# The adaLN modulation moved from VectorE to TensorE in a two-layer hybrid decoder trunk

## The reference

```
c_act = jax.nn.silu(c)
for l in range(DEPTH):                                    # DEPTH = 2
    mod = c_act @ ada_w[l] + ada_b[l]                     # (1024) @ (1024 x 6144)
    sh_m, sc_m, g_m, sh_f, sc_f, g_f = jnp.split(mod, 6, axis=-1)
    h = _rmsnorm(x, norm_mix_g[l]) * (1.0 + sc_m) + sh_m
    cols = h @ w_in[l]                                    # three groups of heads
    ...
    mix = jnp.concatenate([y_a, y_b, y_c], axis=-1) @ w_out[l]
    x = x + g_m * mix
    h = _rmsnorm(x, norm_ffn_g[l]) * (1.0 + sc_f) + sh_f
    x = x + g_f * peer_ffn(h, peer_wq[l], peer_subkeys[l], peer_u[l], peer_v[l])
return _rmsnorm(x, final_norm_g)
```

## Time and profile before

| | |
|---|---|
| median of 3 runs | 1839.49 us (1839.48 to 1844.95) |
| profiled execution | 1839.77 us, its span 1837.9 us |
| TensorE clock, mean of what was granted | 0.851 of full speed |
| PE busy | 1314.2 us (72%) |
| DVE busy | 1398.9 us (76%) |
| ACT busy | 663.5 us (36%) |
| DMA | 706.42 MB, mean 384 GB/s |

### The profile page before, as it was taken

The page is one execution under the profiler, slowest core; times in us unless marked ns, Lnnn a source line. Parts: engine busy times, 40 slices in busy tenths (PEclk is TensorE's granted clock), DMA queues, the critical chain, the costliest instruction groups (busy, mean ns, idle before and its releaser), DMA issues.

```text
span 1837.9 us, 26377 instructions
## 1 busy us (share of the span) xinstructions
PE 1314.2 (72%) x9588; PEld 769.6 (42%) x9588; DVE 1398.9 (76%) x3327; ACT 663.5 (36%) x1634; POOL 517.6 (28%) x564
## 2 busy tenths in 40 slices
PE   2768787787877866787877867787877865555554
PEld 2657675453544534453444534443544531111111
DVE  5878588999974747999965748999965769985554
ACT  2313114444832233445732135336732233231112
POOL 2110012232332222232323232232422233343331
PEclk9875688897998987898988978898988977777777
DMA  9993669998999998999999999998999999999996
GB/s 393 421 396 139 229 240 403 401 415 352 361 420 421 421 420 355 383 414 367 400 421 421 420 420 372 393 422 339 378 421 421 421 421 420 404 405 421 421 421 261
DMA packets 97010, 706.42 MB, mean 384 GB/s; under 512 B 10992, under 2 KB 11504, under 8 KB 13296
## 3 DMA queue, kind: packets, MB, share of 16 engines
q0 software_dynamic: 80640, 587.24, 78.6%
q1 hardware_dynamic: 16240, 117.50, 15.7%
HBM read 703.64 MB, written 1.05 MB: 383 GB/s over the span
## 4 chain that ended last, share of the span: by engine, by line
DVE 43%; DMA 28%; PE 18%; issue 6%; ACT 4%; POOL 0%; DVEq 0%; ACTq 0%; POOLq 0%
DMA ringmem<-in_peer_uv_dram,eidx 23%; DVE ringmem L1451 15%; PE psum L785 5%; DMA W<-in_w_groups_dram 3%; PE psum L661 3%; PE psum L420 2%; DMA ringmem<-in_ada_pairs_dram 2%; DVE coef L1464 2%; DVE ringmem L1095 1%; PE psum L648 1%; DVE cand L1166 1%; DVE cand L1168 1%; DVE eid L1169 1%; DVE attn L1237 1%; DVE ast L1238 1%
## 5 line engine op out<-in xcount | busy, mean ns | idle before, releaser
L785 PE MATMUL psum<-ringmem,diag 64*64 64x512 f32 x4096 | 612.6, 724 | 280.8 <-ACT diag L1066 280.5
L387 POOL DMA_INDIRECT ringmem<-in_peer_uv_dram,eidx x512 | 492.0, 961 | 1082.3 <-PE psum L785 967.6
L1451 DVE SCALAR_TENSOR_TENSOR ringmem<-ringmem,psum 128x1024 f32<-128x1024 f32 x512 | 613.1, 1219 | 240.7 <-DMA ringmem<-in_peer_uv_dram,eidx 227.4
L785 PEld LDWEIGHTS psum<-ringmem,diag 64*64 64x64 f32 x4096 | 151.8, 154 | 605.8 <-ACT diag L1066 399.9
L1066 ACT ACTIVATE diag<-K,coef 128x128 f32<-128x128 f32 x512 | 176.5, 393 | 259.3 <-DVE coef L1464 258.9
L1058 ACT ACTIVATE coef<-dots 128x2 f32<-128x2 f32 x256 | 52.0, 203 | 509.9 <-DVE ringmem L1451 509.2
L420 PE MATMUL psum<-hT,W 128*128 128x128 f32 x1344 | 183.8, 298 | 40.4 <-DMA W<-in_w_groups_dram 22.1
L420 PEld LDWEIGHTS psum<-hT,W 128*128 128x128 f32 x1344 | 172.8, 210 | 83.5 <-issue 39.3
L1095 DVE SCALAR_TENSOR_TENSOR ringmem<-ringmem,diag 128x1024 f32<-128x1024 f32 x96 | 115.5, 1223 | 23.6 <-DMA ringmem<-in_ada_pairs_dram 21.4
L661 PE MATMUL psum<-hT,W 128*128 128x128 f32 x1024 | 126.1, 280 | 7.1 <-ACT hT L835 7.1
L661 PEld LDWEIGHTS psum<-hT,W 128*128 128x128 f32 x1024 | 120.1, 195 | 22.3 <-issue 12.2
(11 more groups left out here) (243 smaller groups left out, 1599.9 us busy)
## 6 DMA issues: line engine op xcount, KB each, us to landing
ringmem<-in_ada_pairs_dram POOLq DMA_DIRECT2D x48, 1024.0 KB, 18.4
W<-in_w_pieces_dram SPq DMA_DIRECT2D x48, 1024.0 KB, 9.4
W<-in_w_groups_dram SPq DMA_DIRECT2D x24, 1536.0 KB, 11.6
W<-in_w_groups_dram SPq DMA_DIRECT2D x12, 1024.0 KB, 9.7
ringmem<-in_peer_uv_dram,eidx POOLq DMA_INDIRECT x512, 14.9
W<-in_w_groups_dram SPq DMA_DIRECT2D x4, 1040.0 KB, 9.2
attn<-in_subkeys_t_dram SPq DMA_DIRECT2D x4, 1024.0 KB, 9.4
K<-in_consts_dram SPq DMA_DIRECT2D x1, 1546.0 KB, 18.3
```

What stands on the lines that cost most here:

```text
L387: nc.gpsimd.indirect_dma_start(slot(k), None, rows, bass.IndirectOffsetOnAxis(ap=eidx[:, ph % 2, m:m + 1], axis=0)).then_inc(row_landed[q ...
L785: mm = nc.tensor.matmul(acc_part(r, half), diag[d, k % DIAGS, d], slot(k)[d, D + half * 512:D + (half + 1) * 512], start=(k % SEL == 0), s ...
L1451: ins = v.scalar_tensor_tensor(out=u, in0=u, scalar=1.0, in1=hrep, op0=ALU.mult, op1=ALU.mult, accum_out=dots[:, j:j + 1])
```

## The change

The modulation is computed on PE instead of DVE. The columns of silu(c), now 128 x 8 numbers (`ccol`), stand in the array: for each of the 8 blocks of 128 inputs, one column of c is repeated over 32 columns of the array. A 1 MB slot now holds 128 inputs (partitions) by 2048 outputs; it passes as four matmuls of 512 columns, each in its own group of 32 columns of the array and so on its own 32 partitions of one PSUM bank. Eight slots make a group (`ADA_GROUPS` = 6): 2048 outputs, that is two sections of the modulation. After a group ACT copies the bank to SBUF (`ada_copy`), PE turns it with four 128 x 128 transposes (`ada_turn`), and DVE reads the sums as columns out of PSUM, adds the bias and folds in the gain (`modulation(g)`). The sections now come in the order in which they stand in `ada_w`.

The pace changes with it: 8 slots before segment 2 as before, then 0.5 slot per segment up to 28 (before: 0.65) and 0.9 after (before: 0.5 up to 56, then 0.75). All three engines follow this table in the lead. SP waits for the seventh slot instead of the sixth. c is loaded as 4 KB instead of 512 KB.

```diff
 def lead_pace():
-    due, out = 2.0 * KD, [1] * (2 * KD - 1) + [2]
+    due, out = 1.0 * KD, [0] * 3 + [1] * (KD - 3)
     for seg in range(2, SEGMENTS):
-        due += 1.3 if seg <= 28 else 1.0 if seg <= 56 else 1.5
-        out += [seg] * (int(min(due, ADA_CHUNKS)) - len(out))
-    return out + [SEGMENTS] * (ADA_CHUNKS - len(out))
+        due += 0.5 if seg <= 28 else 0.9
+        out += [seg] * (int(min(due, ADA_SLOTS)) - len(out))
+    return out
...
-        crow = diag[:].rearrange("p a c -> p (a c)")
+        ccol = diag[:, 0, 0:KD]
+        ada_row = diag[:, 1:5, :]
...
-                sp.dma_start(crow, c.broadcast_to([P, D])).then_inc(s["c_in"], 16)
+                sp.dma_start(ccol, c).then_inc(s["c_in"], 16)
...
-                sp.wait_ge(row_landed[5], 16)
+                sp.wait_ge(row_landed[6], 16)
...
-                Pace(mixing(0)).upto(END - 1)
+                def ada(q):
+                    g, k = divmod(q, KD)
+                    if k == 0 and g >= 2:
+                        pe.wait_ge(s["ada_copied"], g - 1)
+                    if q == 0:
+                        pe.wait_ge(s["c_ready"], 1)
+                    pe.wait_ge(row_landed[q % RING], 16 * (q // RING + 1))
+                    for b in range(4):
+                        mm = nc.tensor.matmul(bank[g % 2][32 * b:32 * b + 32, :], ccol[:, k:k + 1].broadcast_to([P, 32]),
+                                              ringmem[:, q % RING, b * 512:(b + 1) * 512],
+                                              start=(k == 0), stop=(k == KD - 1), skip_group_check=True)
+                    mm.then_inc(slot_free[q % RING], 1)
+                def ada_turn(g):
+                    pe.wait_ge(s["ada_copied"], g + 1)
+                    ...
+                    for j in range(4):
+                        tr = nc.tensor.transpose(bank[2 + g % 2][:, j * P:(j + 1) * P], ada_row[:, j, :], ident)
+                    tr.then_inc(s["ada_turned"], 1)
+                lead = Pace(mixing(0))
+                for q in range(ADA_SLOTS):
+                    lead.upto(LEAD[q])
+                    ada(q)
+                    if q == KD - 1:
+                        ada_turn(0)
+                    elif q % KD == 0 and q > KD:
+                        ada_turn(q // KD - 1)
+                lead.upto(LEAD[-1] + 1)
+                ada_turn(ADA_GROUPS - 1)
+                lead.upto(END - 1)
+                pe.wait_ge(s["mod_ready"], ADA_GROUPS)
                 place_h(0)
...
+                def ada_copy(g):
+                    act.wait_ge(slot_free[(KD * g + KD - 1) % RING], (KD * g + KD - 1) // RING + 1)
+                    if g:
+                        act.wait_ge(s["ada_turned"], g)
+                    nc.scalar.activation(ada_row.rearrange("p a c -> p (a c)"), bank[g % 2][:, :], ACT.Copy
+                                         ).then_inc(s["ada_copied"], 1)
...
-                def ada(j):
-                    q, a = divmod(j, 2)
-                    l, r = divmod(j, 6 * KD)
-                    dve.wait_ge(row_landed[q % RING], 16 * (q // RING + 1))
-                    u = ringmem[:, q % RING, a * D:(a + 1) * D]
-                    ins = v.scalar_tensor_tensor(out=u, in0=u, scalar=1.0, in1=crow, op0=ALU.mult, op1=ALU.mult,
-                                                 accum_out=MC[:, l, SECTIONS[r // KD], r % KD:r % KD + 1])
+                def modulation(g):
+                    l, a = g // 3, 2 * (g % 3)
+                    dve.wait_ge(s["ada_turned"], g + 1)
+                    ...
+                    sums = bank[2 + g % 2].rearrange("p (j b c) -> p b j c", j=4, b=4)[:, :, :, 0]
+                    step(v.tensor_tensor(part.rearrange("p (b j) -> p b j", b=4), sums,
+                                         b.rearrange("p (b j) -> p b j", b=4), ALU.add), *told)
+                    if scale:
+                        m = MC[:, l, scale, :]
+                        step(v.scalar_tensor_tensor(out=m, in0=m, scalar=1.0, in1=pcols[:, l, gain:gain + KD],
+                                                    op0=ALU.add, op1=ALU.mult), "mod_ready")
```

82 lines of the change are left out of this document (37 added, 45 removed).

## The result

The changed kernel takes 1851.65 us (median of 5 runs, 1850.61 to 1855.50) against 1840.29 for the kernel before (5 runs, 1839.48 to 1844.95): a ratio of 1.0061, with a 95% interval from 1.0045 to 1.0078. It is slower, by 11 us. The forecast was 1822 us, 17 us faster. Run once more on another chip, beside 27 runs of the kernel before (median 1841.30), the same kernel took 1847.22 us (10 runs, 1840.67 to 1852.64): ratio 1.0035, interval 1.0018 to 1.0052. So both times slower, by 6 to 11 us, and with a scatter of 12 us that the experiments explain only in part.

A forecast was written before the change was run, and what follows sets the result against it. The experts' rows bound the phases, so the lead's gain arrives one for one. Terms -0.5, -6, -12, -2.5, +1.5, +2.5 sum to -17.0 us: 1822 us, range 1806 to 1860 (the forecast's own 1806 to 1834).

The forecast's parts named there:

- The first step: Whole kernel: expert rows bound the phases, so what the lead gains or loses arrives at the end one for one.
- the price of a slot: On PE: a slot's four column groups run side by side, costing 1.1 us, or 2.0 at half clock.
- an extra for the change of shape: On PE: a drain per tiling-mode change, estimated 0.15 us each, 7 us over 25 slots; left out of the sum.
- Rivals 2 and 3: Lead: PE at half clock, 125 to 200 us, 1862, chance 0.12; slot's matmuls one after another, 1878, chance 0.08.
- Rival 1: Attention segments keep their pace, set by the loop over three engines; sum -7, 1833 us; chance 0.20.
- 123.2 to 183.8, -12: Lead's attention stretch, the largest term: segments fall from 4.43 to 3.5 us; -12.0 us in sum.
- The -3.8 for full clock behind the segments: Behind the attention segments: products with the values and the last levels go at full clock, -3.8 us.
- Twice ACT's copy and PE's turn stand in the way, +1.5: In the attention stretch: ACT's copy and PE's turn of a group's sums stand in the way twice, +1.5 us.
- why the clock should be 1.00: Attention segments: slots' 512-column products, 1.1 us in 3.5, raise PE's granted clock from 0.50 to 1.00, as in the next phase.
- 37.65 to 123.2, -6: From first to last projection: slots +5.5, DVE's chunks off the chain -5.3, clock -2.2 and -1.5, transfers -2.5; sum -6.0 us.
- The -2.2 for the clock of the last group: Among the projections: 16 matmuls after a wait took 5.97 us, 3.73 without; slots in such waits give -2.2 us.
- The -2.5 for transfers: Among the projections: 4 MB of slot loads move behind the last group's load, -2.5 us, bounds 0 and -9.5.

The follow-up runs named there:

- e5_paced: The changed kernel with the first nine expert gathers issued at most three ahead; 1840.34 us, ratio to the kernel before 1.0005.
- e7_late_paced: The changed kernel with turns two and additions three slots later, and first gathers at most three ahead; 1830.85 us, ratio to the kernel before 0.9956.
- e4_late: The changed kernel with the modulation's turns two slots later on PE and additions three slots later on DVE; 1835.34 us, ratio to the kernel before 0.9965.
- e1_repeat: The changed kernel once more, unaltered, on another chip; 1847.22 us.
- e11_double: The changed kernel with gathers at most three ahead, and every modulation slot but the first eight multiplied twice; 1863.36 us.
- e8_fewer: The changed kernel with half as many modulation slots among the projections, the others later; 1839.25 us.
- e12_all: The changed kernel with gathers paced, turns and additions late, and fewer slots among the projections; 1827.34 us, ratio to the kernel before 0.9929.
- the third edit: Pace table of the changed kernel cut from 0.5 to 0.25 slot per segment up to 28, so fewer slots among the projections; alone 1839.25 us.
- e13_six: The changed kernel with the first nine expert gathers at most six ahead; 1846.83 us.
- e14_dve_burst: The changed kernel, gathers in a burst, with a 1.22 us reduction on DVE beside each slot but the first eight; 1857.28 us.

## Why the prediction was wrong

The first step, that the lead's end arrives one for one, held within the scatter: the rest is 1552 to 1558 us in the seven profiles of the table. So did the price of a slot, 1.1 us at full clock (measured 1.06) and 2.0 at half (1.93). To leave out an extra for the change of shape was right too: from a slot's start to the next product of another shape it is 1.00 us (159.14 to 160.14), and whole segments of 3.44 us hold two such changes. The Trainium skill, TensorEngine Tiling (Array Packing), Key Properties, says that a change of mode drains TensorE; no separate cost of it can be seen here. Rivals 2 and 3 fell: the clock between 150 and 175 us was 0.91, with two segments at half instead of more than six, and a slot took no 3.7 us. Rival 1 fell in its reason: the segments did speed up. The table compares the steps with the profile after and with e5_paced, where the stall is away.

| step | forecast | after | paced |
|---|---|---|---|
| start to first projection | -0.5 | -0.2 | -0.3 |
| to the last projection | -6.0 | +3.2 | -1.4 |
| to L596 | -12.0 | -0.4 | -0.5 |
| to the queries (two steps) | -1.0 | -3.8 | -1.7 |
| to place h | +2.5 | +10.7 | +2.0 |
| sum | -17.0 | +9.5 | -1.8 |

**The step that failed with the largest sum is "123.2 to 183.8, -12".** Its segments at 3.5 us were right where they ran undisturbed. In the changed kernel, from the first scores (132.77) to the levels at 170.48 it is 37.7 us, where before it was 40.6 (128.79 to 169.41): -2.9 over nine segments that at 3.44 each should have given 8.9. The missing 6 are in the three segments named above. 138.85 to 144.87 is 6.0 us, with the slot and turn on PE, ACT's copy ahead of it, and DVE, which in its own order stands 2.45 us before the addition while its copies for the next segment are behind it; and 144.87 to 154.92 is two segments in 10.05 us, at half clock. The -3.8 for full clock behind the segments didn't come either: the stretch from 170.48 to 186.40 took 15.9 us, more than the 14.4 before, because the second group's end lies there.

Two terms of this step failed. The first is the turn: "Twice ACT's copy and PE's turn stand in the way, +1.5" said nothing of what queues behind DVE's addition. Twice DVE stands there, 2.45 and 5.70 us, and PE after it 1.77 and 2.23. e7_late_paced puts the price of this term within the step at 7.3 us (e4_late 5.8), and over the whole kernel at 9.5 to 11.9. The second is the clock: "why the clock should be 1.00" held for the segments from 154.92 on and for those before 144.87, but two between them ran at half clock, 3.2 us, and kept doing so with the turns late. The count was off as well: nine segments lie between the two marks, not twelve, so 0.99 us each gives 8.9 and not 11.2. The slots at the front were right, +1.1 by the trace (forecast +1.5).

**The step "37.65 to 123.2, -6" gave -1.4 with the stall away, and +3.2 in the first profile after.** Even the same program scatters here: 88.7 us after, 84.9 in the repeat. Five slots at 1.1 were charged, 5.5 us; e11_double puts the 12 slots there at 6.9, so that charge was 1.4 too low. The -2.2 for the clock of the last group isn't safe either: its 16 matmuls took 5.32 us in the trace after, behind a wait of 4.24, and 3.84 in e5_paced, behind one of 1.71. The -1.5 for dv came (2.10 and 3.49 us instead of 7.12). The -2.5 for transfers can't be read apart: e8_fewer agrees with its direction, since fewer slots freed among the projections let the weight groups come sooner, but the fewer loads of the change against the kernel before didn't carry the step to -6. In the trace after, the slots at 61.95, 67.61 and 72.37 push the end of group v from 70.3 to 75.4 us, hence the load of dq and PE's wait for it, 4.46 us at 86.05; before, PE waited 2.17 us just ahead of that place, for DVE. DVE's chunks left the chain, but PE's slots took their place in it: 8.1% by line from 37 to 126 us, where DVE's chunks had 6.1% from 37 to 124.

**The stall was in no step.** It cost 6.9 us by medians. No rival had it, and nothing in the trace before shows it: there GpSimd issued its gathers in a burst as well and PE's heads went on. With the stall gone the changed kernel equals the kernel before (1.0005), so about 7 of the 11 us of the first result, or all 6 of the second, are the stall, and the gain of 17 us was lost before it: by the runs 9.5 us to group ends, and 3.5 more to the placing of the slots (e12_all against e7_late_paced).

**Is the idea then bad?** No: e12_all, the change with three edits in order and pace, is 0.7% faster than the kernel before: 13.9 us of the 17 that were forecast. That the three edits bring this back is shown by the runs. Their parts don't add: apart they gave -6.9, -11.9 and -8.0 us against the changed kernel, together -19.9. One overlap is seen: the third edit alone also shortened the stall (2.75 us instead of 5.20), and with the stall gone it gives 3.5. Nor do the 13.9 us bear out the forecast's steps: against the kernel before they are -8.7 to the last projection (forecast -6), -9.4 to L596 (-12), -3.2 to the queries (-1) and +7.8 to place h (+2.5).

**Open.** What PE or its signal waits for in the stall. Shown is that it needs the burst (gone with three ahead, there with six or nine), that in the changed kernels it sits at the first head to end once five or more gathers were issued and not at one that ended with four, and that neither PE's place in its program nor DVE's load matters. In six of nine profiles q_out arrived within 0.1 us of a signal from a landing gather (in e1_repeat at 269.70 with such signals from 269.66 on, in e13_six at 271.34 with one at 271.28), but in e14_dve_burst (276.56) none was within 0.5 us, so that isn't the rule. And the kernel before issued eight gathers by 277.3 us, one of them landed by 272.8 and a second by 278.5, while its head that ended at 278.1 passed. Why not there wasn't found. Nor was what lowers the clock in the two segments behind the first group's end.
